# Four weight remainders of the query projection computed on VectorE instead of GpSimd, at the start of an expert gather

## What is computed

```python
def chunk_fn(hc):                                   # 128 tokens x 1024
    q = (hc @ w_query).reshape(TOKEN_CHUNK, PEER_HEADS, 2, PEER_HALF)
    sc = jnp.einsum('thpd,pnd->thpn', q, sub_keys).astype(jnp.float32)
    vals, idx = lax.top_k(sc, PEER_TOPK)            # 16 of 128, twice
    ...
    top_s, pos = lax.top_k(cand, PEER_TOPK)         # 16 of the 256 pairs
    expert_idx = jnp.take_along_axis(cand_idx, pos, axis=-1)
    gate = jax.nn.softmax(top_s, axis=-1)
    u = expert_u[expert_idx]
    act = jax.nn.gelu(jnp.einsum('thkd,td->thk', u, hc).astype(jnp.float32), approximate=False)
    vv = expert_v[expert_idx]
    return jnp.einsum('thk,thkd->td', (gate * act).astype(hc.dtype), vv)
```

## Time and profile before

| | us |
|---|---|
| median of 3 runs | 2595.02 |
| lowest and highest | 2592.16 and 2595.42 |
| the profiled execution, its own time | 2597.78 |
| its span in the trace | 2596.0 |
| PE busy in the span | 2229.3 |
| DVE busy | 1703.7 |
| ACT busy | 866.8 |
| POOL busy | 864.0 |
| gathers: data moved by queue q0 | 536.90 MB |
| weights and all else moved by queue q1 | 143.49 MB |

### The profile page before, as it was taken

The page is one execution under the profiler, slowest core; times in us unless marked ns, Lnnn a source line. Parts: engine busy times, 40 slices in busy tenths (PEclk is TensorE's granted clock), DMA queues, the critical chain, the costliest instruction groups (busy, mean ns, idle before and its releaser), DMA issues. The chain is left out here.

```text
span 2596.0 us, 33131 instructions
## 1 busy us (share of the span) xinstructions
PE 2229.3 (86%) x11846; PEld 1394.7 (54%) x11846; DVE 1703.7 (66%) x3855; ACT 866.8 (33%) x1931; POOL 864.0 (33%) x649
## 2 busy tenths in 40 slices
PE   8998999889987788877777777777779999989999
PEld 7886667765542333323332222223257777776787
DVE  7998797348676777766676667766544644456553
ACT  3222762333232342322232222322224222246431
POOL 0001213345444355534434344334313211212243
PEclk9999999999999999999999999999989999989999
DMA  4332215279999999999999999999922212232253
GB/s 146 106 110 94 78 50 179 73 267 414 421 421 419 421 420 419 413 421 415 419 417 418 417 409 417 415 408 411 420 74 90 85 62 73 88 126 94 84 196 106
DMA packets 131074, 682.50 MB, mean 263 GB/s; under 512 B 13536, under 2 KB 23136, under 8 KB 65120
## 3 DMA queue, kind: packets, MB, share of 16 engines
q0 software_dynamic: 73728, 536.90, 50.1%
q1 hardware_dynamic: 57184, 143.49, 15.8%
HBM read 655.70 MB, written 24.64 MB: 262 GB/s over the span
## 5 line engine op out<-in xcount | busy, mean ns | idle before, releaser
L1664 PE MATMUL bank<-peer_uv,peer_diag 128*128 128x512 f32 x2048 | 975.9, 622 | 284.6 <-ACT peer_diag L1323 279.6
L1557 DVE SCALAR_TENSOR_TENSOR peer_uv<-peer_uv,early_h 128x1024 f32<-128x1024 f32 x512 | 644.2, 1269 | 387.2 <-DMA peer_uv<-in_peer_uv,peer_index 382.9
L1664 PEld LDWEIGHTS bank<-peer_uv,peer_diag 128*128 128x128 f32 x2048 | 387.0, 197 | 834.4 <-issue 831.0
L1358 POOL DMA_INDIRECT peer_uv<-in_peer_uv,peer_index x512 | 535.1, 1045 | 742.9 <-PE bank L1664 654.0
L223 POOL TENSOR_TENSOR weight_low<-weight_ring,weight_high 128x1024 fp32r<-128x1024 f32 x102 | 248.8, 2439 | 680.3 <-ACT weight_high L206 680.3
L155 PE MATMUL bank<-hT_high,weight_high 128*128 128x512 f32 x952 | 403.0, 423 | 14.3 <-POOL weight_low L223 5.1
L156 PE MATMUL bank<-hT_low,weight_high 128*128 128x512 f32 x952 | 375.8, 395 | 0.0
L157 PE MATMUL bank<-hT_high,weight_low 128*128 128x512 f32 x952 | 375.3, 394 | 0.0
L206 ACT ACTIVATE weight_high<-weight_ring 128x1024 fp32r<-128x1024 f32 x171 | 180.9, 1058 | 468.9 <-PE bank L157 456.0
L1318 ACT ACTIVATE peer_gelu<-peer_dots 128x2 f32<-128x2 f32 x256 | 52.0, 203 | 798.3 <-DVE peer_uv L1557 798.2
L155 PEld LDWEIGHTS bank<-hT_high,weight_high 128*128 128x128 f32 x952 | 181.9, 191 | 66.5 <-issue 19.0
(11 more groups left out here) (416 smaller groups left out, 2740.0 us busy)
## 6 DMA issues: line engine op xcount, KB each, us to landing
weight_ring<-in_weights SPq DMA_DIRECT2D x171, 512.0 KB, 3.4
z_store<-fill_stage SPq DMA_DIRECT2D x70, 256.0 KB, 2.3
peer_uv<-in_peer_uv,peer_index POOLq DMA_INDIRECT x512
merge_z<-z_store SPq DMA_DIRECT2D x8, 768.0 KB, 6.0
merge_z<-z_store SPq DMA_DIRECT2D x12, 512.0 KB, 4.4
score_store<-peer_work SPq DMA_DIRECT2D x16, 192.0 KB
peer_sc<-score_store SPq DMA_DIRECT2D x24, 128.0 KB
swz<-z_store SPq DMA_DIRECT2D x1, 2560.0 KB, 9.5
```

The lines of the kernel that those rows point to most:

```text
L1358: pool.indirect_dma_start(uv[:, p % SLOTS], None, peer_uv, bass.IndirectOffsetOnAxis(index[:, n % 2, p % TOPK:p % TOPK + 1], 0)).then_inc( ...
L1557: nc.vector.scalar_tensor_tensor(uv[:, p % SLOTS, 0:D], uv[:, p % SLOTS, 0:D], 1.0, h2[:, t], ALU.mult, ALU.mult, accum_out=dots[:, p % TO ...
L1664: mm = nc.tensor.matmul(bank[2 * (t % 2) + c][:], diag[:, p % SLOTS], uv[:, p % SLOTS, D + c * 512:D + (c + 1) * 512], start=(p % PICKS == ...
```

## The change

A table `LOWS_BESIDE` names low parts that DVE makes in the first head: units 6 and 7 in group 0, unit 8 in group 1, unit 9 in group 2, in each case after the two dots and after some steps of `ahead`, and ahead of `weigh`. GpSimd issues groups 0 to 4 with no low part between them and takes up its low parts with unit 10. `self.lows` only counts in Python.

```diff
-        self.lows = u + 1
+        self.lows = max(self.lows, u + 1)
...
+LOWS_BESIDE = {0: (EARLY - 2, EARLY - 1), 1: (EARLY,), 2: (EARLY + 1,)}
...
             def _(pool):
                 for n in range(2, EARLY - 2):
                     w.low_part(pool, nc.gpsimd, u0 + n)
-                lows = EARLY - 2
+                lows = EARLY + 2
                 for g, n, q, t in groups():
-                    if 0 < g and lows < EARLY + 2:
-                        w.low_part(pool, nc.gpsimd, u0 + lows)
-                        lows += 1
-                    elif lows < QUERIES + 2 and query_group(lows - 2) + RINGS + 2 <= g or (
+                    if lows < QUERIES + 2 and query_group(lows - 2) + RINGS + 2 <= g or (
...
                         next(ahead, None)
                         next(ahead, None)
+                        for u in LOWS_BESIDE.get(q, ()):
+                            w.low_part(dve, nc.vector, u0 + u)
```

## The result

| | before | after |
|---|---|---|
| median of 8 runs each, us | 2595.22 | 2603.07 |
| lowest and highest | 2590.17 and 2598.54 | 2599.03 and 2606.95 |
| ratio of the times, 95% interval | | 1.0031, 1.0019 to 1.0042 |
| the profiled execution, its own time | 2597.78 | 2600.06 |
| its span in the trace | 2596.0 | 2598.2 |

The changed kernel is 0.31% slower: 7.9 us, with an interval of 4.9 to 10.9. The forecast was 2599.6 in a range of 2594.5 to 2605.0. The time lies inside the range. The case called the likeliest, no change within 0.2%, did not come: the measured ratio is above it, and only the low end of its interval (1.0019) reaches it.

The account below looks back on a forecast made before the run. The prediction took the DMA engines moving the gathers to bound the stage. Full again 12.5 us later, less 6.2 and 1.7 us of work already moved, gave +4.6 on 2595.0: 2599.6 us, range 2594.5 to 2605.

Parts of the forecast that it names:

- The case called the likeliest: Whole kernel: time unchanged within 0.2%, 5.2 us; chance 0.62.
- Filling the two holes is worth at most 4.0 us: DMA engines at the stage's start: not full in 546 to 554 and 564 to 573, missing 1.3 and 2.7 us.
- Ten gathers in a row, PE starved of unit 6: GpSimd issues groups 0 to 4 until 555; PE gets low part 6 late and stands for 7.7 us.
- the sum of 9.5: PE's loss up to unit 7: 7.7 us standing for unit 6 plus 1.8 us for its slow start.
- The load of unit 9 sets the gelu: Unit 9's load, sharing DMA with gathers, takes 11.8 us; its high part starts at 573.3 against 567.86.
- Rival 1: Weight loads not held up, PE alone sets the gelu at 574.8: +2.6, 2597.6 us; chance 0.20.
- The gelu 5.4 us later: First gelu on ACT, behind unit 9's high part: moves from 571.36 to 576.8.
- 6.75 us from gelu to group 5: Time from first gelu to GpSimd's issue of group 5, taken unchanged from before; puts the issue at 583.55.
- 12.5-6.2-1.7 = 4.6: Stage: DMA engines full again 12.5 us later, less 6.2 for early gathers and 1.7 for unit 11 with its store.
- Low parts 8 and 9 on DVE cost nothing: DVE before the weights of groups 1 and 2: 1.22 us each, covered by PE's pace; 0, at most 2.4 us.
- Rival 2, not slower: PE not late enough, gelu stays at 571.36, only the filled queue counts: -0.8, 2594.2 us; chance 0.12.
- Rival 3, +7.4 to +9.8: Unit 9's load stuck until 576, low parts 8 and 9 lose cover: 2602.4 to 2604.8 us; chance 0.23.

Follow-up runs that it names:

- before, load first: Against the kernel before, SP issues each weight load ahead of the score store it stood behind; ratio 0.9996.
- 6 and 7 ahead, load first: Against the changed kernel, low parts 6 and 7 on DVE ahead of the first dots, each weight load ahead of its score store; ratio 0.9992 to before.
- 6 ahead, load first: Against the changed kernel, low part 6 on DVE ahead of the first dots, each weight load ahead of its score store; ratio 1.0004 to before.
- 6 and 7 ahead, twice: Against the changed kernel, low parts 6 and 7 on DVE ahead of the first dots, loads still behind score stores; ratios 1.0020 and 1.0005 to before.
- 6 ahead: Against the changed kernel, low part 6 on DVE ahead of the first dots, the rest unchanged; ratio 1.0022 to before.
- 8 and 9 on GpSimd: Against the changed kernel, low parts 8 and 9 back on GpSimd ahead of groups 3 and 4; ratio 1.0013 to before.
- 6 and 7 on GpSimd: Against the changed kernel, low parts 6 and 7 back on GpSimd ahead of groups 1 and 2; ratio 1.0020 to before.
- changed, twice: The changed kernel, and the same kernel timed and profiled once more without an edit; ratio 1.0031 to before both times.
- changed, warm PE: Against the changed kernel, five dummy identity products on PE ahead of group 0, into a bank nobody reads; ratio 1.0027 to before.
- gelu ahead, twice: Loads ahead of stores, group 0's gelu earlier in ACT's queue; low parts 6 and 7 on DVE ahead of dots, or all on GpSimd: 0.9983, 0.9990.

## Why the prediction was right or wrong

One table holds the argument. Where group 5 goes out, after the first gather, and how long the stage lasts:

| kernel | group 5 | stage | stage less group 5 | GB/s, first 60 us |
|---|---|---|---|---|
| before, load first | 32.22 | 1352.4 | 1320.2 | 390 |
| 6 and 7 ahead, load first | 32.07 | 1353.6 | 1321.5 | 388 |
| before | 35.35 | 1355.1 | 1319.8 | 368 |
| 6 ahead, load first | 35.49 | 1355.4 | 1319.9 | 370 |
| 6 and 7 ahead, twice | 35.85, 35.75 | 1354.4, 1355.3 | 1318.6, 1319.6 | 368, 363 |
| 6 ahead | 37.42 | 1356.9 | 1319.5 | 357 |
| 8 and 9 on GpSimd | 38.84 | 1358.7 | 1319.9 | 344 |
| 6 and 7 on GpSimd | 39.51 | 1359.5 | 1320.0 | 342 |
| changed, twice | 41.04, 41.64 | 1360.7, 1361.6 | 1319.7, 1320.0 | 328, 325 |
| changed, warm PE | 39.16 | 1361.9 | 1322.7 | 334 |
| gelu ahead, twice | 23.79, 27.62 | 1349.7, 1349.6 | 1325.9, 1322.0 | 401, 400 |

For group 5 between 32 and 42 the stage follows it one for one, within some 1.5 us, whatever was done to get there (the warm PE is the exception). By the time its rows move, those of groups 0 to 4 are through, or nearly so, and what is left to do from then on is the same in every version. Where ten gathers went out in a row and group 5 came later than 35, the DMA engines stood nearly empty ahead of it. In the kernel before they did not: it had lost its time earlier, when groups 3 and 4 came late. That the two losses give the same line is in part chance.

The last column is the more direct test, of the mean rate of the DMA engines over the first 60 us after the first gather's issue. Each 1 GB/s less than before, over 60 us, is 60/418 = 0.14 us of work not yet done, and this gives the difference of the stages from that of before within 1 us, but for two: "6 and 7 ahead, load first" (2.9 us shorter by the sum, 1.5 by the stage) and the warm PE (4.9 and 6.8 us longer). With the gelu ahead the queue doesn't run dry at all: 4.7 and 4.6 us by the sum, 5.4 and 5.5 measured. These are the shortest stages seen here.

By the prediction's steps:

- **Filling the two holes is worth at most 4.0 us:** too small, and not the point. The changed kernel filled the second hole, and the first in one execution of two, and gained nothing, since all ten early gathers are through before group 5's come. The version with the gelu ahead leaves the first hole as it was (352 GB/s in 545 to 553) and yet gained 5.4 us of stage: 9 x (422-294)/422 = 2.7 from the second, and 27 x (423-406)/423 = 1.1 from the stretch behind it, which the prediction had called full. By the mean over 60 us it is 4.7 in all. The rest, 0.7, is within what two executions of one kernel differ by, 0.9.
- **Ten gathers in a row, PE starved of unit 6:** right. Low part 6 on DVE began at 554.16, 12.8 us after the first gather against a forecast of 13.6. PE took up unit 6 7.0 us later, not 7.7, and unit 6 ran slow as said: 0.63 us a product at first and 0.39 at its end, in a stretch with a mean granted clock of 0.66, a mixture of 2.4 and 1.2 GHz. From unit 6's first product to unit 7's it took 564.34-555.42 = 8.92 us instead of 6.37. So the slow start cost 2.55, not 1.8, and the sum of 9.5 came out as forecast because the two errors cancel, which is luck.
- **The load of unit 9 sets the gelu:** right, and it is the load and not PE by little (29.73 against 28.75, and 30.48 against 29.12). Unit 8 landed 18.5 us after the first gather (issued at 543.95, 15.9 us to landing), inside the forecast of 17.0 to 19.5. In 555 to 561 of the changed kernel the two queues had these packets, one for one as in the earlier trace rows:

```profile
q0 software_dynamic: 272, 1.97, 77.9%
q1 hardware_dynamic: 273, 0.54, 23.0%
```

  A store and a unit took 11.0 to 11.3 us in four runs, where 11.8 was forecast; in the changed kernel it was 11.2, and 11.6 in its second execution. The Trainium skill, DMA: Bandwidth & Descriptors, section Queues, rings and completion order, says that an engine drains a whole packet, typically of 9 to 17 descriptors, from one queue before it switches. The trace doesn't bear this out for this pair of queues: in slices of 2 us, from 547.35 to 565.35, the two counts never lie more than 7 apart (112 and 112, 97 and 98, 100 and 107 are three of the nine). Batches of 9 or more in turn, on each of 16 engines, would by estimate not come out so even. Rival 1, which needed nearly two small pieces for one row, fell.
- **The gelu 5.4 us later:** right within the scatter of two executions, +4.64 and +5.39. Unit 9 was put at 30.4 after the first gather and came at 29.7 and 30.5.
- **6.75 us from gelu to group 5:** mis-sized, 7.8. It was copied from the kernel before, group 0 with its 5.44 us included, and the eight records took 6.49 and, in the second execution, 6.34. The idle time ahead doesn't explain it: it was shorter than before (4.68 and 5.06 us, against 7.28). What was longer is the part of group 0 that ran at the lower clock. Here is a stretch of after, with 0.50, 1.2 GHz:

```profile
576.00:581.00 5.00, 5.00 (x7) 1.90 (x7) 5.00 (x15) 0.90 (x3) 0.00 (x0) 0.50 0.14 56
```

  In slices of 1 us the clock is back at 1.00 at about 581.3, 5.7 us after group 0 began; before, it was back at 576.0, 3.6 us after. The prediction had this effect at unit 6 and took it as unchanged here. At group 5 this and the gelu's earlier place cancel: +5.7 measured, +5.4 forecast.
- **"12.5-6.2-1.7 = 4.6":** mis-sized by 1.0, the part of the miss that the stage shows. "The queue does not run dry again" was wrong: behind the hole the engines moved 370 GB/s in 585 to 600. The same stretch of before:

```profile
585.00:600.00 15.00, 15.00 (x49) 8.45 (x48) 12.88 (x45) 7.65 (x17) 6.82 (x7) 1.00 1.00 401
```

  15 x (401-370)/418 = 1.1 us, which is the term that was missing (the second execution of the changed kernel moved 369 at the same distance from its first gather, 583.55 to 598.55). A group needs 5.0 us of DMA and PE sends the next in 4.8, so a queue that starts empty has nearly nothing in store, and every small wait shows.
- **Low parts 8 and 9 on DVE cost nothing:** right in the changed kernel. PE went from group 0 to unit 8 without idle time, and groups 5 and 6 are 4.81 us apart as before. It holds because PE is slow there. With a warm PE it waited 0.40 us for low part 8.
- **Rival 2, not slower:** fell. **Rival 3, +7.4 to +9.8:** its time is near the measured 7.9, its mechanism did not come: unit 9 landed at 30, not at 33, and low parts 8 and 9 kept their cover.

Of the 7.9 us between the medians, the stage accounts for 5.6 and, in the second profiled execution, 6.5. The rest, about 2 us, isn't seen in any stage of the two traces: in these two executions the changed kernel was even shorter outside the stage, which is why its profiled execution was only 2.3 us longer than that of before. The interval of the ratio reaches down to 4.9, and ratios scatter around their stages in the other versions too (with 6 and 7 ahead 1.0020, 5.2 us, beside a stage 0.7 us shorter), so there may be nothing more. That is left open. The likeliest case failed although the chain was right, because +4.6 stood so near the bound of 5.2 that 1 us of missed terms was enough to cross it: a chance of 0.62 for no change within 0.2% claimed more than a sum with such terms can. And part of what brought 4.6 so near to the 5.6 of the stage is luck, since the slow start of unit 6, the slow group 0 and the earlier load missed in both directions.

## What to carry to other kernels

Where DMA bounds a stage, look first for the moment from which its queue is never empty again, and follow back what releases the transfer that ends the hole: here a gelu behind other work in ACT's in-order queue. Issuing the transfers ahead of the hole earlier gained nothing here, and it delays the small loads that share the engines, in this case by their number of pieces times a large row's time. Before an operation is moved to an idle engine, hold its new place against the moment its consumer needs it, not against the idle time; and when two causes stand within 1 or 2 us of each other, undoing one shows little.

## What the runs showed of the hardware

- **A long instruction that DVE is running holds up GpSimd's issue of a gather until it is done.** An issue takes 0.94 us. Beside a low part on DVE (540.47 to 541.70) it took 1.91 us, from 540.59 to 542.50, so it ended 0.80 us after DVE was done. In the changed kernel the last gather's issue (553.22 to 554.26) ended 0.8 us after a dot of 552.24 to 553.45. A dot that begins after the issue leaves it alone: the eighth issue, 550.22 to 551.16, took 0.94 with a dot from 550.88. The Trainium skill, SBUF — State Buffer, section Terms, says that the loser of the port pair blocks for the whole instruction, and the trace agrees with its numbers. That the port pair is the reason here no run shows. The prediction looked for such blocks at the low parts only and priced none at the new place; here that delay helped.
- **What an idle PE costs afterwards goes by how long the clock stays low in the new work, not by how long PE was idle.** In the eleven traces where PE had been idle before group 0 for 3.7 to 13.1 us, the group began with the granted clock at 0.50 (1.2 GHz), which lasted from 2.95 to 6.13 us. The group took 5.13 to 6.72 us: in each of the eleven the 3.65 us of a fast group and half of that stretch, within 0.05. The idle time before doesn't order them. The longest, 13.10 us, goes with 2.95 and 5.13, and 6.17 us with 6.13 and 6.72. Where PE had been idle for about 1 us or less, in three traces, the group took 3.60 to 3.67.
- **A small transfer among gathers is priced in pieces, not in bytes.** A score store and a weight unit are 512 pieces and 0.72 MB, and they took 11.0 to 11.6 us whenever rows were waiting, against 5.5 where the gathers ran dry. In a gap between gathers 383 to 422 small pieces went through in 2 us.
